# Hybrid Fourier / pooling / latent-attention step: the next head's first scores and maxima in places behind the prompt tile's, keys before queries, later query weights by GpSimd

## The reference, cut to what matters

```python
q = (_rmsnorm(q_lat, w['q_norm_g']) @ w['w_q_up']).reshape(B, L, N_HEADS, QK_NOPE + QK_ROPE)   # 8 heads, 64 + 32
...
q_rope = _apply_rope(q_rope, cos[:, None, :], sin[:, None, :])      # latent tokens only
...
kv = (ckv_all @ w['w_kv_up']).reshape(B, Lk, N_HEADS, QK_NOPE + V_DIM)
...
s = jnp.einsum('bqhd,bkhd->bhqk', qblk, k) * scale
p = jax.nn.softmax(s, axis=-1)
o = jnp.einsum('bhqk,bkhd->bqhd', p, v)
```

## Time and profile before

| | |
|---|---|
| median of 3 runs | 2217.21 us (2217.01 to 2218.97) |
| the profiled execution's own time | 2216.42 us |
| its span, first to last instruction | 2214.3 us |
| granted TensorE clock, mean | 0.994 |
| attention pipeline of layer 0 | about 302 to 628 us |
| attention pipeline of layer 1 | about 1381 to 1708 us |
| PE busy | 2133.8 us, 96% of the span |

### The profile page before, as it was taken

One profiled execution on the slowest core, in us unless ns is written; L12 is line 12 of the kernel. 1 busy time (PEld: TensorE's weight loads), 2 busy tenths in 40 slices (PEclk: granted clock), 3 DMA queues, 4 the chain that ended last, 5 costly groups with the idle time before them and its releaser, 6 DMA issues.

```text
span 2214.3 us, 36107 instructions
## 1 busy us (share of the span) xinstructions
PE 2133.8 (96%) x13185; PEld 2033.8 (92%) x13185; DVE 1074.1 (49%) x2775; ACT 887.3 (40%) x2223; POOL 732.0 (33%) x656
## 2 busy tenths in 40 slices
PE   6999999999999999999999999999999999999997
PEld 4899888888899999999989998888888999999997
DVE  2441268888764668663162314888886111120213
ACT  2421267787831212113152214787787122111312
POOL 1323133443422234333441312343443123433242
PEclk9999999999999999999999999999999999999999
DMA  9811000000353333324255100000014111111232
GB/s 280 266 30 31 26 1 1 2 1 2 121 156 86 93 84 101 81 64 144 73 194 163 40 1 25 2 1 1 2 35 171 48 37 48 43 46 39 63 124 86
DMA packets 194622, 155.68 MB, mean 70 GB/s; under 512 B 8636, under 2 KB 186000, under 8 KB 193424
## 3 DMA queue, kind: packets, MB, share of 16 engines
q1 hardware_dynamic: 194448, 153.38, 22.6%
HBM read 124.89 MB, written 28.48 MB: 69 GB/s over the span
## 4 chain that ended last, share of the span: by engine, by line
PE 85%; DVE 6%; ACT 4%; issue 3%; DMA 1%; POOL 0%; SPq 0%; DVEq 0%; POOLq 0%; ACTq 0%
PE ps L1625 24%; PE ps L1627 23%; PE ps L1626 23%; PE ps L1817 5%; PE ps L1842 3%; PE ps L1843 2%; DVE partmax L1467 1%; DVE probsT L1480 1%; ACT probs L834 1%; PE ps L1635 1%; ACT probsT L850 1%; DMA raw<-in_w_mod 1%; PE ps L1860 1%; DVE xn_high L1226 1%; PE ps L1821 1%
## 5 line engine op out<-in xcount | busy, mean ns | idle before, releaser
L1625 PE MATMUL ps<-xn_high,split_br 128*128 128x384 f32 x1584 | 531.7, 336 | 0.0
L1627 PE MATMUL ps<-xn_high,split_br 128*128 128x384 f32 x1584 | 529.4, 334 | 0.0
L1626 PE MATMUL ps<-xn_low,split_br 128*128 128x384 f32 x1584 | 529.3, 334 | 0.0
L967 ACT ACTIVATE sigmoids<-ps 128x384 f32<-128x384 f32 x144 | 70.4, 492 | 613.1 <-PE ps L1627 613.1
L1009 POOL TENSOR_TENSOR split_br<-raw,split_br 128x1024 fp32r<-128x1024 f32 x82 | 198.0, 2416 | 320.4 <-ACT split_br L695 320.4
L1626 PEld LDWEIGHTS ps<-xn_low,split_br 128*128 128x128 f32 x1584 | 297.5, 188 | 0.0
L1625 PEld LDWEIGHTS ps<-xn_high,split_br 128*128 128x128 f32 x1584 | 297.4, 188 | 0.0
L1627 PEld LDWEIGHTS ps<-xn_high,split_br 128*128 128x128 f32 x1584 | 297.4, 188 | 0.0
L1480 DVE TENSOR_TENSOR probsT<-ps,probsT 128x384 fp32r<-128x384 f32 x384 | 213.3, 556 | 74.9 <-ACT sum_inv_rows L857 36.4
L834 ACT ACTIVATE probs<-ps,negmax 128x384 f32<-128x384 f32 (+1 forms) x400 | 229.7, 575 | 38.2 <-DVE negmax L1473 37.6
L850 ACT ACTIVATE probsT<-ps 128x384 fp32r<-128x384 f32 x384 | 188.8, 492 | 67.7 <-PE ps L1817 40.3
(11 more groups left out here) (228 smaller groups left out, 4156.8 us busy)
## 6 DMA issues: line engine op xcount, KB each, us to landing
raw<-in_w_in SPq DMA_DIRECT2D x74, 512.0 KB, 4.0
raw<-in_w_mod SPq DMA_DIRECT2D x48, 512.0 KB, 5.3
park_high<-xn_high SPq DMA_DIRECT2D x6, 1536.0 KB, 6.2
park_low<-xn_low SPq DMA_DIRECT2D x6, 1536.0 KB, 10.6
xn_high<-park_high SPq DMA_DIRECT2D x2, 4608.0 KB, 15.9
rows<-in_x_sample SPq DMA_DIRECT2D x16, 512.0 KB, 6.9
raw<-in_w_out SPq DMA_DIRECT2D x16, 512.0 KB, 6.6
rows_mid<-rows SPq DMA_DIRECT2D x9, 512.0 KB, 2.6
```

The lines of the kernel that those rows point to most:

```text
L1625: mm(out, wh, xh, start=first, stop=False)
L1626: mm(out, wh, xl, start=False, stop=False)
L1627: return mm(out, wl, xh, start=False, stop=last)
```

## The change

Four things change.

1. **Slots.** `score_slot(s, c)` and `max_slots(s)` say which score and which maximum stand in a place of step s. For j = 0 to 6 nothing changes. In step j = 7 the places after the prompt tile's score, which were empty, take the first two scores of the next head's tile 0; in step j = 8 only its third score is left. The maxima follow: prompt and (m, 0) in step 7, (m, 1) and (m, 2) in step 8.
2. **Keys before queries.** `beside` gives the keys in steps 1, 2, 3 and the queries in steps 4, 5, 6.
3. **Query weights of heads 2 to 7 by POOL**, in step j = 7 behind whatever POOL has in that step, with a wait for the last use of the buffer. DVE no longer makes them within the attention.
4. **Fewer pieces.** The sign of the rotation goes into the table `q_scale`, so a head's weights are three pieces instead of five (`head_columns`), and both parts of each are a plain copy and a plain subtraction.

```diff
+def score_slot(s, c):
+    h, j = divmod(s, TT)
+    if j < TT - 2:
+        return (s + 1, c) if s + 1 < TILES else None
+    m = (h + 1) * TT
+    slots = [(m - 1, 0), (m, 0), (m, 1)] if j == TT - 2 else [(m, 2), None, None]
+    return slots[c] if slots[c] and slots[c][0] < TILES else None
+
+def max_slots(s):
+    h, j = divmod(s, TT)
+    m = (h + 1) * TT
+    if j == TT - 2:
+        slots = [(s, 2), (m - 1, 0), (m, 0)]
+    elif j == TT - 1:
+        slots = [None, (m, 1), (m, 2)]
+    else:
+        slots = [(s, 2) if j or not s else None, (s + 1, 0), (s + 1, 1)]
+    return [it if it and it[0] < TILES else None for it in slots]
...
-        return [("qk"[n // 3], h + 1, n % 3)]
+        return [("kq"[n // 3], h + 1, n % 3)]
...
+            def head_weights(h):          # on GpSimd
+                own_done()
+                done["wq_ready"] = l * HEADS + h + 1
+                filled(pool, l, "attn", attn[("q", h - 2, 2)])
+                for hi, lo, src in head_columns(h):
+                    ins = g.tensor_copy(hi, src)
+                ins.then_inc(S("wq_high"), 1)
+                pool.wait_ge(S("wq_high"), l * HEADS + h + 1)
+                for hi, lo, src in head_columns(h):
+                    ins = g.tensor_tensor(lo, src, hi.bitcast(F32), ALU.subtract)
+                ins.then_inc(S("wq_ready"), 1)
...
+                if j == 7 and h + 2 < HEADS:
+                    head_weights(h + 2)
...
-                if j == 7 and h + 2 < HEADS:      # on VectorE
-                    head_weights(h + 2)
-                    head_weights_low(h + 2)
...
-                    if what == "max" and s + 1 < TILES and c < parts(s + 1) - 1:
-                        maxes(s + 1, c)
+                    if what == "max" and max_slots(s)[1 + c]:
+                        maxes(*max_slots(s)[1 + c])
...
-                    if what == "score" and s + 1 < TILES and c < parts(s + 1):
-                        scores(s + 1, c)
+                    if what == "score" and score_slot(s, c):
+                        scores(*score_slot(s, c))
```

More of the change, by code:

```diff
@@ L93, in make_tables @@
     q_scale[NOPE:NOPE + ROPE, :LAT] = cos.T
-    q_scale[NOPE + ROPE:, :LAT] = sin.T
+    q_scale[NOPE + ROPE:, :LAT] = (sin * sign).T
     q_scale *= (NOPE + ROPE) ** -0.5
@@ L487, in split_dest, with head_columns @@
         return bs[:, 4 + d if d < 2 else d - 2]
+    def head_columns(h):
+        u, c0 = h % 2, h * (NOPE + ROPE)
+        yield wq[:, u, :, 0:NOPE + ROPE], wq_low[:, u, :, 0:NOPE + ROPE], wq_raw[:, :, c0:c0 + NOPE + ROPE]
+        for a2 in range(2):
+            cols = slice(NOPE + ROPE + 16 * a2, NOPE + ROPE + 16 * a2 + 16)
+            src = wq_raw[:, :, c0 + NOPE + 16 * a2:c0 + NOPE + 16 * a2 + 16]
+            yield (wq[:, u, :, cols].rearrange("p k (f e) -> p k f e", e=8),
+                   wq_low[:, u, :, cols].rearrange("p k (f e) -> p k f e", e=8),
+                   src.rearrange("p k (f e) -> p k f e", e=8)[:, :, ::-1, :])
     def raw_unit(n):
@@ L629, in _ @@
             sp.dma_start(chan_dft[:], tab["chan_dft"]).then_inc(S("dft_in"), 16)
-            filled(sp, l, "attn", attn[("k", HEADS - 1, 2)])
+            filled(sp, l, "attn", attn[("q", HEADS - 1, 2)])
             load_units(sp, unit_at[("gate", l, 0)], unit_at[("gate", l, 1)] + 1)
@@ L881, in beside_high @@
                     o = K_PLACES[i]
-                    act.wait_ge(S("q_low"), (l * HEADS + h) * 3 + (3 if h else 0))
+                    act.wait_ge(S("q_low"), (l * HEADS + h) * 3)
                     if i == 2:
@@ L1331, in _ @@
             ins.then_inc(S("lat_ready"), 1)
[L1333 to L1344, removed]
-                ins.then_inc(S("wq_high"), 1)
[L1347 to L1363, removed]
+            low_done(dve, NCH * KF * (l + 1))
+            for h in range(2):
+                for hi, lo, src in head_columns(h):
+                    ins = v.tensor_copy(hi, src)
+                ins.then_inc(S("wq_high"), 1)
             def pool_edges(kt):
@@ L1422, in _ @@
                     .then_inc(bank_free[b], 1)
-            head_weights_low(0)
-            head_weights_low(1)
+            for h in range(2):
+                dve.wait_ge(S("wq_high"), l * HEADS + h + 1)
+                for hi, lo, src in head_columns(h):
+                    ins = v.tensor_tensor(lo, src, hi.bitcast(F32), ALU.subtract)
+                ins.then_inc(S("wq_ready"), 1)
             for n in range(4):
@@ L1440, in query_values @@
                 if i == 0:
-                    dve.wait_ge(S("k_low"), (l * HEADS + h) * 3 + (0 if h else 3))
+                    dve.wait_ge(S("k_low"), (l * HEADS + h) * 3 + 3)
                 sl = slice(i * CH, (i + 1) * CH)
@@ L1506, in _ @@
             for s in range(STEPS):
+                if max_slots(s)[0]:
+                    maxes(*max_slots(s)[0])
                 if s < TILES:
-                    maxes(s, parts(s) - 1)
                     negmaxes(s)
@@ L1518, in _ @@
                                 query_values(hh, i)
-                    if what == "max" and s + 1 < TILES and c < parts(s + 1) - 1:
-                        maxes(s + 1, c)
+                    if what == "max" and max_slots(s)[1 + c]:
+                        maxes(*max_slots(s)[1 + c])
                     if what == "low" and turned(s - 1, c) is not None:
                         turned_low(s - 1, turned(s - 1, c))
-                h, j = divmod(s, TT)
-                if j == 7 and h + 2 < HEADS:
-                    head_weights(h + 2)
-                    head_weights_low(h + 2)
             unmix(*mixed_in(STEPS - 1))
```

## The result

The changed kernel takes 2197.8 us (median of 4 runs, 2197.6 to 2198.4) where the kernel before took 2217.2: a ratio of 0.9912, 95% interval 0.990 to 0.9925, 19.4 us less. The forecast was 2191, range 2175 to 2206. The direction and the gaps that would go were right; the gain is three quarters of the forecast's 26 us.

The account below looks back on a forecast made before the run. PE, busy 96% of the span, bounds the kernel; only its standstills, mostly at head boundaries, can be won. 2216.4 - 34.2 + 6.3 + 1.6 = 2190.1 us, forecast 2191 as the median is 0.8 higher; range 2175 to 2206 (own range 2183 to 2199).

Parts of the forecast that it names:

- Where the time goes; which gaps: PE's idle time sits at 14 head boundaries; gaps of 0.56 (unmix) and 0.97 us (late keys) go.
- The boundary's gain, 2.5 us (12 times) and 2.1 (twice): Head boundaries: slots, weights and keys together shorten the 12.44 us stretch to 9.75 to 9.9; sum 34.2 us.
- the third gap: PE's 0.87 us loss at a boundary, ahead of group 3's mixing, to DVE's unmix; about 0.6 stays.
- PE's pure work in the stretch is about 9.0: Boundary stretch of 12.44 us: three big gaps are 2.4 us, smaller ones about another 1, leaving about 9.0 of work.
- DVE's work is the floor: Boundary stretch: DVE has 9.1 us of work left, level with PE's 9.0, so the gain is at most 3.3 us.
- Weights on POOL at nothing: POOL's six instructions a head take about 1.9 us, at most 4.8, behind waits that cover them, so cost nothing.
- The cover of up to 7 us: Weights beyond about 7 us make group 2's gates late for ACT; each us over costs one at 12 boundaries.
- The two engines side by side: POOL's new work lengthens nothing on DVE; if overlap blocked, DVE would be held 1.9 us at 12 boundaries, 23 us.
- The weights' share: Boundary gain is 2.5 us at the 12 where DVE made weights, 2.1 at the two behind head 6, without weights.
- Keys first, 7.9 us: Steps 1 to 6: about 1.05 us of PE work moves; cost 6.3 us in heads 2, 4, 6 and 1.6 in others.
- Fewer pieces at the start, the last head: Heads 0 and 1: fewer weight pieces win nothing; last head's earlier prompt maximum, under 0.3 us twice, taken as 0.
- rival 2: Boundary backlog moves instead of going: only gaps of 1.5 us go, swap costs 8, 2204 us; chance 0.23.

Follow-up runs that it names:

- keys_alone: Kernel before, with keys made before queries; slots as before, weights on DVE as before but in six pieces instead of ten: 2209.3 us, ratio 0.9967.
- slots_and_weights: Changed kernel with queries before keys, as in the kernel before; new slots and weights on POOL kept: 2271.3 us, ratio 1.0253.
- slots_and_keys: Changed kernel with weights of heads 2 to 7 on DVE at the end of step 7, in six pieces: 2198.3 us, ratio 0.9918.
- dve_order: Changed kernel with DVE, in step 8, doing the next tile's negated maximum and group 2's unmix ahead of tile 7's last low part: 2196.9 us, ratio 0.9913.
- lift_early: Changed kernel with DVE's step 8 negation and unmix ahead of the last low part, and ACT's lift ahead of its last high part: 2194.6 us, ratio 0.9905.
- x3: Changed kernel with each head's query weights made three times on POOL: 2197.2 us, ratio 0.9912.
- x5: Changed kernel with each head's query weights made five times on POOL: 2217.5 us, ratio 1.0001.
- values_later: Changed kernel; heads 2, 4, 6: ACT copies values behind the next step's lift and first exponential, POOL takes gates before values: 2196.6 us, ratio 0.9911.

## Why the prediction was right, and where its size was off

- **Where the time goes; which gaps.** Right: 14 boundaries, and the gaps of 0.56 and 0.97 us gone. That keys made last cause the second, which the view called "issue", is shown by keys_alone, which takes it away and gains 7.3 us net of the swap (1.10 us at the boundaries behind head 6, which hold no weights), and by slots_and_weights, where the wait follows the keys to 3.75 us.
- **The boundary's gain, 2.5 us (12 times) and 2.1 (twice).** This is the term that was mis-sized: the stretches became 1.94 and 1.59 us shorter, in all 26.5 us for 34.2, and that is the whole of the miss. In the stretch of the earlier trace rows, 12.44 to 10.52 us, 0.58 us are missing: 0.27 for the wait at the second transposes, for the bank of the query third that DVE now scales in step 7, which I had not foreseen; 0.21 because the third gap is 0.81 and not 0.6; and 0.1 for the rest. Two steps of the working failed. First, "PE's pure work in the stretch is about 9.0": I took the gaps of 0.1 us for losses, but they stand in the stretch after as before, for instance behind each set of the last transposes, and 10.52 less its two waits is 9.4. Second, "DVE's work is the floor", "DVE and PE are level": slots_and_keys gives DVE 1.0 us more here and the boundary stays at 15.1. What holds up the mixing of group 3 is a chain from PE's last transposes through ACT's high part, row sums and lift to DVE's low part, negation and `unmix`; dve_order and lift_early shorten it, and the gap goes to 0.56 and 0.40. I had the wait's place and its last link right and its cause wrong.
- **Weights on POOL at nothing.** Right, and closely: 0.65 and 1.02 us for the three copies and the three subtractions, 1.8 together for my 1.9. The cover of up to 7 us was too small rather than too large: 6.2 us are free (x3), and 10.5 us (x5) cost 20 us where 12 x 3.5 = 42 would follow from 7. With 1.65 us of cost at 10.5, I estimate that it ends near 9 us.
- **The two engines side by side.** DVE's low part of the probabilities is still 545 to 560 ns in all 384 cases (`L1507 DVE TENSOR_TENSOR probsT<-ps,probsT x384: 545/558/560`). That agrees with the row and with the Trainium skill's rule in "SBUF — State Buffer", "Who interferes with whom", as I used it.
- **The weights' share.** 12 x 0.4 = 4.8 us of my 34 was the difference between boundaries with and without DVE's weights, and in the full change it is 12 x 0.35 = 4.2. Measured alone the move is worth 3.5 us, behind keys first 7, and with slots and keys nothing. The gains don't add, since the slots leave DVE an idle place that six pieces fit into. What the fewer pieces and what the move to POOL are worth was not told apart.
- **Keys first, 7.9 us.** Measured 7.5, in part by luck. With the 0.15 us of step 6, even heads cost 0.95 for my 1.05, odd ones 0.3 for 0.2, and head 0, which I had put with the odd ones, gains 0.1. But the work that moves is not 1.05 us: by the starts a third of the queries takes PE 1.04 us and the thirds of the keys 0.70, 0.35 and 0.70, so it is 3 x 1.04 - 1.75 = 1.37, of which steps 1 to 4 of head 0 give back 1.08. In the even heads that nothing comes back in steps 1 to 3 was right; ACT's order is the cause of 0.3 us of it, by values_later, and the rest is open. ACT's wait for the gates there, which I saw growing from 0.54 to 1.3 us, is 0.60: everything is 0.8 us later, as forecast, but ACT too.
- **Fewer pieces at the start, the last head.** The last head is 0.4 us longer in one layer, taken as 0. No run changes the pieces alone.

Of the cases, the forecast's mechanism came, with a part of rival 2 in it: the third gap did stay.

## What to carry to other kernels

Before moving work into an empty place, look for the data that it waits for: the same slots are worth 4 us with the keys ready and cost over 50 without. An engine that waits for another has room even where its busy time nearly fills a stretch; whether it is the floor is told by giving it more work, not by adding up its rows. And when a wait is shortened, name the next one at the same place: 0.4 us taken out of a gap left 0.15, and 0.25 left 0.04.

## What the runs showed of the hardware

- TensorE's granted clock fell behind long stands, but not behind all of the same length. Behind stands of 3.75 to 4.0 us (slots_and_weights) it went to 0.50, that is 1.2 GHz of 2.4, at all 14 boundaries, and was whole again 3 to 6 us after PE had started again. Behind twelve stands of 1.5 to 2.5 us (pool_weights_x5) it fell three times, each time behind one of 2.2 us, and stayed 1.00 behind others of 2.2 us. Behind the waits of about 1 us of the kernel before it stayed 1.00 at every boundary. It also fell at one of six heads in values_later, where waits of at most about 0.9 us stand close together:

```profile
1613.00:1616.00 3.00, 1.63 (x11) 1.08 (x10) 2.19 (x5) 2.98 (x10) 2.39 (x1) 0.96 0.00 0
1616.00:1618.00 2.00, 2.00 (x10) 1.90 (x8) 1.23 (x7) 1.27 (x5) 1.71 (x3) 0.50 0.00 0
```

- If the 1.25 us a boundary in slots_and_weights are all the clock's, each microsecond of waiting cost about 1.45 us there (4.0 for 2.75).
- The same subtraction of weights on DVE costs 0.775 us beside POOL and 0.344 alone. Within the attention of slots_and_keys, with POOL idle, it takes at most 0.359, and together with two of 32 columns 0.56.
